# One z slot of the delta mixer computed together with the decay inputs, ahead of the mixer's rounds

## The reference, cut to what matters

```
x = rms_norm(x, norm_out_g)                        # end of the first block
h = rms_norm_2(x, g_mix)
proj = h @ w_in                                    # 1024 x 8224
glu_a, glu_b, q, k, v, z, a_in, b_in, gate_a, gate_b = split_cols(proj, IN_SIZES)
...                                                # short convolution and silu of q, k, v
g = -exp(a_log) * softplus(a_in + dt_bias)         # 2 x 8 decay inputs a token
beta = sigmoid(b_in)                               # 2 x 8 more
o = gated_delta_rule(forwards) + gated_delta_rule(backwards)   # 8 heads of 128
o = rms_norm_2(o, delta_norm_g) * silu(z)          # z: 1024 columns
```

## Time and profile before

| | us |
|---|---|
| median of three runs | 1200.44 (1199.74 to 1205.01) |
| the profiled execution, its own time | 1202.45 |
| its span, first to last instruction | 1200.5 |

### The profile page before, as it was taken

The page is one execution under the profiler, slowest core; times in us unless marked ns, Lnnn a source line. Parts: engine busy times, 40 slices in busy tenths (PEclk is TensorE's granted clock), DMA queues, the critical chain, the costliest instruction groups (busy, mean ns, idle before and its releaser), DMA issues.

```text
span 1200.5 us, 21345 instructions
## 1 busy us (share of the span) xinstructions
PE 1170.7 (98%) x8592; PEld 1087.1 (91%) x8592; DVE 839.9 (70%) x1519; ACT 700.9 (58%) x1181; POOL 324.8 (27%) x257
## 2 busy tenths in 40 slices
PE   8999999999999999999999999999999999999997
PEld 7777899998887799998899999999989989999886
DVE  6796588884675578885558787888854656555456
ACT  5475576663467576664466666776666445444344
POOL 1172200000027300000157667576555220000010
PEclk9999999999999999999989999999999999999999
DMA  7633355545543365555333332332323646555542
GB/s 286 251 141 140 128 211 207 195 181 204 179 183 133 120 246 211 209 184 213 134 141 140 107 133 98 124 125 87 105 72 108 226 176 221 209 186 201 202 154 82
DMA packets 31587, 199.74 MB, mean 166 GB/s; under 512 B 4289, under 2 KB 6481, under 8 KB 8706
## 3 DMA queue, kind: packets, MB, share of 16 engines
q1 hardware_dynamic: 29506, 189.27, 44.1%
q0 software_dynamic: 1840, 8.60, 1.8%
q10 hardware_dynamic: 144, 0.52, 0.1%
HBM read 197.33 MB, written 1.05 MB: 165 GB/s over the span
## 4 chain that ended last, share of the span: by engine, by line
PE 83%; DVE 9%; ACT 4%; issue 2%; POOL 1%; DMA 0%; SPq 0%; POOLq 0%; ACTq 0%; DVEq 0%
PE ps L1185 24%; PE ps L1187 23%; PE ps L1186 23%; PE ps L1562 1%; PE ps L1578 1%; DVE ps L2837 1%; PE ps L1339 1%; PE ps L1358 1%; DVE conv L2768 1%; PE ps L1326 1%; DVE wlo L2382 1%; PE ps L1210 1%; PE ps L1279 1%; DVE x L2511 1%; PE ps L1584 0%
## 5 line engine op out<-in xcount | busy, mean ns | idle before, releaser
L1185 PE MATMUL ps<-halves,whi 128*128 128x256 f32 x1472 | 411.1, 279 | 0.1
L1186 PE MATMUL ps<-halves,whi 128*128 128x256 f32 x1472 | 406.0, 276 | 0.0
L1187 PE MATMUL ps<-halves,wlo 128*128 128x256 f32 x1472 | 406.0, 276 | 0.0
L2382 DVE TENSOR_TENSOR wlo<-raw,whi 128x2048 fp32r<-128x2048 f32 (+1 forms) x133 | 300.6, 2263 | 116.1 <-ACT whi L1842 112.9
L1842 ACT ACTIVATE whi<-raw 128x2048 fp32r<-128x2048 f32 (+1 forms) x143 | 269.4, 1886 | 96.7 <-PE ps L1187 91.4
L1185 PEld LDWEIGHTS ps<-halves,whi 128*128 128x128 f32 x1472 | 283.8, 193 | 0.8 <-DVE halves L2976 0.5
L1187 PEld LDWEIGHTS ps<-halves,wlo 128*128 128x128 f32 x1472 | 283.8, 193 | 0.0
L1186 PEld LDWEIGHTS ps<-halves,whi 128*128 128x128 f32 x1472 | 283.8, 193 | 0.1
L1109 POOL TENSOR_TENSOR wlo<-raw,whi 128x1024 fp32r<-128x1024 f32 x72 | 172.4, 2404 | 53.4 <-ACT whi L1851 52.9
L1001 POOL TENSOR_TENSOR rstd<-sumsq,half_power 128x1 f32<-128x1 f32 x14 | 11.5, 824 | 573.2 <-ACT xn L1869 405.7
L1185 PE MATMUL ps<-whi,halves 128*128 128x512 f32 (+4 forms) x440 | 148.5, 337 | 4.1 <-DVE halves L2485 3.2
(11 more groups left out here) (337 smaller groups left out, 1847.0 us busy)
## 6 DMA issues: line engine op xcount, KB each, us to landing
raw<-in_stream SPq DMA_DIRECT2D x176, 1024.0 KB, 4.8
gain<-in_gains POOLq DMA_DIRECT2D x7, 512.0 KB, 6.0
bias<-in_rel POOLq DMA_DIRECT2D x1, 1536.0 KB, 8.4
raw<-in_stream SPq DMA_DIRECT2D x2, 648.0 KB, 7.3
cst<-in_consts POOLq DMA_DIRECT2D x1, 1280.5 KB, 9.1
raw<-in_stream SPq DMA_DIRECT2D x2, 528.0 KB, 4.4
x<-in_x SPq DMA_DIRECT2D x2, 512.0 KB, 4.3
out<-xn SPq DMA_DIRECT2D x4, 256.0 KB, 2.4
```

The source lines that it names most:

```text
L1185: nc.tensor.matmul(out, a_hi, b_hi, start=start, stop=False)
L1186: nc.tensor.matmul(out, a_hi, b_lo, start=False, stop=False)
L1187: return nc.tensor.matmul(out, a_lo, b_hi, start=False, stop=stop)
L2382: dve.tensor_tensor(used(wlo, n), used(raw, n), used(whi, n).bitcast(F32), ALU.subtract)\
```

## The change

The slot `z0` (256 columns of w_in) and the 32 decay columns become one matrix of 288 columns, in two "columns" slots of 512 rows each, `("z_decay", 0)` and `("z_decay", 1)`. They stand where `ab` stood. The number of slots stays the same. Its products are 48 matmuls of 288 columns, into bank 4 (t = 0) and bank 5 (t = 1). `decay_inputs` reads columns 256 to 287 of the two banks; the tanh and product of z0 (`first_z`) are issued in tick 7 of round 0 on ACT and DVE. The order of the other slots moves up, so that round 4 has three slots.

The splits move with it: ACT and DVE split one slot more in `norm_behind_down(4)`, DVE both halves of the new matrix ahead of the addition for t = 1 and its half of the first q-k slot at the very end; POOL's half of that slot comes behind both deviations and two memsets.

```diff
-    plan.append(("narrow", "ab", ("w_in_2", 0), 6144, 32))
+    rows_major("z_decay", ("w_in_2", 0), [(5120, 2 * P), (6144, 32)])
...
-    other = [glu[0:2], [z[0]] + glu[2:4], [glu[4], z[1]], [z[2], glu[5], z[3]], [glu[6], gates[0]],
+    other = [glu[0:2], glu[2:4] + [z[1]], [glu[4], z[2]], [glu[5], z[3], gates[0]], [glu[6]],
              [glu[7]] + gates[1:2], gates[2:3], gates[3:5]]
...
 POOL, double norm:
             for t in range(TT):
                 deviation(4, t)
                 deviation_5(t)
-                if t == 0:
-                    split_shared(("qk", 0))
             pool.memset(sum_row[:, :].bitcast(F32), 0.0).then_inc(*S["rows_cleared"].one("mixer"))
             pool.memset(glu_in[:, :, :], 0.0).then_inc(*S["glu_cleared"].one())
+            split_shared(("qk", 0))
...
 PE, in place of ab_products:
+            def first_z_and_decay_products(t):
+                for half in range(2):
+                    n = slot_of[("z_decay", half)]
+                    if t == 0:
+                        wait_low(pe, n)
+                    wait_split(5, t, (half,))
+                    wh, wl = used(whi, n), used(wlo, n)
+                    for i in range(4):
+                        kt = 4 * half + i
+                        last = three(ps[:, 4 + t, 0:Z_DECAY], xhi[:, kt, t * P:(t + 1) * P], xlo[:, kt, t * P:(t + 1) * P],
+                                     in_order(wh[:, i, :]), in_order(wl[:, i, :]), kt == 0, kt == KT - 1)
+                    if t:
+                        last.then_inc(*S["weights_used"].one(n))
...
             def level_turn(h):
                 pe.wait_ge(*S["inverse_begun"].at(h))
+                if h == 0:
+                    pe.wait_ge(*S["tanh_used"].at(("z", 0)))
...
 ACT, norm_behind_down:
                 split(last + 3)
                 round_turned(5 if k == 4 else k, [(1, 0), (1, 1)])
+                if k == 4:
+                    split(last + 4)
...
 DVE, norm_behind_down:
                 normalize(after, [0])
                 split(last + 1)
-                if k == 2:
+                if k in (2, 4):
                     split(last + 2)
                 add_to_x(k, last, 1)
...
                 lows(after, [(1, 0), (1, 1)])
+                if k == 4:
+                    split(last + 3)
...
 DVE, in tick 7 of round 0 (ACT makes the tanh before it):
+            def first_z():
+                dve.wait_ge(*S["tanh_made"].at(("z", 0)))
+                dve.scalar_tensor_tensor(xn[:, :, 0:TOK], tanh[:, TANH_OF[("z", 0)], :].rearrange("p (t c) -> p t c", t=2), 1.0,
+                                         ps[:, 4:6, 0:2 * P], ALU.add, ALU.mult).then_inc(*S["tanh_used"].one(("z", 0)))
```

More of the change, by code:

```diff
@@ L175, in pack_stream @@
                 out[n].reshape(P, KT, 2 * P)[:] = evens_first(out[n].reshape(P, KT, 2 * P))
-        elif kind == "narrow":
-            a, c = args
-            out[n].reshape(P, KT, 256)[:, :, 0:c] = w[:, a:a + c].reshape(KT, P, c).transpose(1, 0, 2)
         elif kind == "down":
@@ L547 @@
 AB_SPINS = (6, 2)
+Z_DECAY = 2 * P + 32
 END_SPINS = (5, 8)
@@ L556 @@
 NORMS = len(GAINS) - 1
-MIX_SLOTS = [("ab", -1, 0)] + [(slot[0], r, 2 * i) for r, slots in enumerate(ROUNDS) for i, slot in enumerate(slots)] \
+MIX_SLOTS = [(("z", 0), -1, 0)] + [(slot[0], r, 2 * i) for r, slots in enumerate(ROUNDS) for i, slot in enumerate(slots)] \
     + [(("delta_out", i), len(ROUNDS), 0) for i in range(KT // 2)]
@@ L580, in finished_slot @@
     return slot_at(r, i - 1) if i else slot_at(r - 1, TICKS - 1)
+FIRST_Z_AT = (0, 7)
 def tanh_order():
@@ L590, in tanh_order @@
                 order.append(key)
+            if (r, i) == FIRST_Z_AT:
+                order.append(("z", 0))
             if r < HEADS and i == 3:
@@ L820, in weights_of @@
                 return at.rearrange("p (k c) -> p k c", k=4)[:, :, 0:sum(c for _, c in entry[3])]
-            if entry[0] == "narrow":
-                return at.rearrange("p (k c) -> p k c", k=KT)[:, :, 0:entry[4]]
             return at
@@ L1772, in _ @@
                 turn_norm(5, t)
-                ab_products(t)
+                first_z_and_decay_products(t)
                 if t == 0:
@@ L2052, in up2 @@
                     .then_inc(*S["p_high"].one())
+            def first_z():
+                act.wait_ge(*S["weights_used"].at(slot_of[("z_decay", 1)]))
+                act.wait_ge(*tanh_free(TANH_BEFORE[("z", 0)]))
+                act.activation(tanh[:, TANH_OF[("z", 0)], :].rearrange("p (t c) -> p t c", t=2), ps[:, 4:6, 0:2 * P], ACT.Tanh,
+                               scale=0.5).then_inc(*S["tanh_made"].one(("z", 0)))
             def evacuate(key):
@@ L2296, in _ @@
                         evacuate(finished_slot(r, i))
+                    if (r, i) == FIRST_Z_AT:
+                        first_z()
                     if r < HEADS and i == 3:
@@ L2713, in decay_inputs @@
             def decay_inputs():
-                dve.wait_ge(*S["weights_used"].at(slot_of["ab"]))
+                dve.wait_ge(*S["weights_used"].at(slot_of[("z_decay", 1)]))
                 dve.wait_ge(params2_loaded, 16)
-                link(dve.tensor_copy(ab[:, 0, :, :], ps[:, 3, 0:64].rearrange("p (t c) -> p t c", t=2)))
+                link(dve.tensor_copy(ab[:, 0, :, :], ps[:, 4:6, 2 * P:Z_DECAY]))
                 dt = row_at["dt_bias_2"].unsqueeze(1).broadcast_to([P, TT, 16])
@@ L3027, in _ @@
             decay_inputs()
-            split(slot_of["ab"] + AHEAD)
+            split(slot_of[("z_decay", 1)] + AHEAD)
             for r in range(len(ROUNDS)):
```

## The result

The changed kernel is slower by 0.2%: 1206.06 us median of 20 executions against 1203.36 us for 20 of the kernel before, ratio 1.0021 [1.0012, 1.0031]. The forecast was 1197.7, with 1193.5 to 1202.5 as its range. It was wrong: in size and in sign against the kernel before.

A forecast was written before the change was run, and what follows sets the result against it. PE, busy 98% of the span, was taken as the bound. Norm with clock -0.8, z0's tanh and product +0.6, rounds 4 and 5 -2.5 sum to -2.7 us: 1197.7 us against the median, range 1193.5 to 1202.5.

The forecast's parts named there:

- The fall of the clock over t = 0: Double norm: one short clock fall after PE's 3.45 us idle stretch, costing 1.1 us, within bounds of 0 and 7 us.
- Part 4: Round 0, tick 7: z0's tanh and product added on ACT and DVE delay round 1; +0.6 us, from 0 to +0.69.
- Part 5: Rounds 4 and 5: round 4 loses a slot, round 5 gives some back; together -2.5 us, from -1.85 to -2.6.
- What hides the moved splits: Double norm: the moved q-k and v0 splits finish before PE wants them; v0 hidden by 1.8 us, no cost.
- What follows is a chain of latencies ... and moves along with it: From qk0's end to the next transposes: the chain shifts with qk0's end, keeping the 1.9 us full-clock gain.
- Part 3, the clock: Double norm: PE's idle stretch may lower the clock; 1.1 us taken, leaving -0.8 us for norm with clock.
- What would show it: Signs of error: matmul above 0.13 us, late q-k split, over 0.7 us extra round 1 wait, rounds 4-5 saving outside 1.5-4.
- PE starves at the norm and the clock falls for good: Double norm: first product 2.25 us late, half clock through both tiles; +2.5 us in all, 1202.9 us; chance 0.15.
- rival 3: Another name for "PE starves at the norm and the clock falls for good", the slower case; 1202.9 us, chance 0.15.

The follow-up runs named there:

- e6_first_spins: Changed kernel with only 14 spins on PE ahead of the t = 0 products at the double norm; ratio to the kernel before 0.9998.
- e2_rounds_only: Kernel before's double norm with the changed kernel's slot order in the rounds, z0 left out altogether; ratio to the kernel before 0.9985.
- e8_act_tail: Changed kernel plus 14 and 3 spins; ACT makes decay logarithms and evacuates qk0 before its half roundings, one POOL half split a tick later; ratio to before 1.0031.
- e9_tail: e7_late_half with qk0 evacuated ahead of glu0's second half, glu1's first-half remainders on DVE after the gating, three spins less; ratio to before 0.9961.
- e7_late_half: Changed kernel with DVE's split of the new matrix's second half behind t = 1's first gain, and spins at both waits; ratio to before 0.9977.
- e4_spins: Changed kernel with 14 spins ahead of the t = 0 products and 9 ahead of PE's wait for the first gated projection; ratio to before 0.9987.
- e5_wide_ab: Kernel before with its decay matmuls 256 columns wide instead of 32, the further columns unread; ratio to before 1.0005.
- e1: Changed kernel's double norm with the kernel before's rounds; z0 computed in the norm unread, and again in round 1; ratio to before 1.0040.
- e3: Changed kernel with ACT's decay logarithms a tick earlier and both halves of glu0's rounding behind qk0's evacuation; ratio to before 1.0056.
- e12: e9_tail run again unchanged, on one chip with e11; 1197.22 us, ratio to the kernel before 0.9955.
- e11: Kernel before with 256-column decay matmuls, spins ahead of the gated-projection wait and e9_tail's two tail moves, without the change; 1198.11 us, ratio 0.9959.

## Why the prediction was wrong

**Right.** The 288-column matmuls go in steps of 0.1225 us (609.00 to 611.45 us is twenty steps); 0.123 was forecast. PE's first product came at T + 4.42, 2.18 later than before; forecast 2.25, by the two splits on DVE (2.62 us; forecast 2.70). The row of after:

```profile
595.92 2.62 DVE L2396 TENSOR_TENSOR wlo<-raw,whi 128x1152 fp32r<-128x1152 f32 x2
```

The fall of the clock over t = 0, held possible behind the long idle stretch, came: the products took from 600.49 to 605.17, and e6_first_spins puts its cost at 1.04 us; forecast 1.1. Up to qk0's end the norm gained 0.9 us against before; forecast 0.8. This gain is the second low stretch of the earlier trace rows, which did not come over qk0 again; in e2_rounds_only an unchanged norm has only one such stretch, so the gain depends on the execution compared with. POOL's half of the q-k slot took 2.60 us, not the long 4.20, and was done at 608.24, ahead of PE's want at 611.57.

"Part 4" said +0.6: +0.32. DVE comes with the first `prod` of round 1 0.6 us later, and PE's wait at L1565 is 1.00 against 0.39; half of that is made up within the round. "Part 5" said -2.5: round 4 gave 2.49, round 5 took 0.80 back, together -1.69, just outside the bounds of -1.85 to -2.6; the missing part is in round 4, forecast at -2.9 to -3.7.

**Wrong, first step.** "What hides the moved splits" said of v0: ACT rounds it at 607.5 to 609.4, hidden by 1.8. It was held against PE's want of v0 alone. It came at 610.36 and hid there, but it pushed all that stands behind it in ACT's list: glu0's half, the three table loads, glu0's other half, qk0's evacuation. The sentence "What follows is a chain of latencies ... and moves along with it" assumed that PE's end of qk0 starts this chain; after the change ACT's queue does. Worth: PE 0.9 ahead at qk0's end, 0.74 behind at L1493, so 1.6 us. That it is this queue is shown by e8_act_tail, where the evacuation goes ahead of the halves and the same transposes come 1.51 us earlier; e9_tail against e7_late_half (0.94 us, with the evacuation and one remainder moved and three spins less) agrees. How the 1.6 divide between v0's rounding and the order of glu0's halves wasn't tried alone, and is argued from the rows.

**Wrong, second step.** "Part 3, the clock" looked for falls in the norm and priced one. It missed that a new wait at L1493 is also an idle stretch. The clock fell behind it for 6.9 us; from L1493 to round 1's turn PE took 21.77 us, before 18.59: +3.18. e4_spins and e6_first_spins show it: the same wait with spins in it costs 1.58 us less even where the fall was already halved. None of the signs that "What would show it" gave for being wrong came true (0.1225 us a matmul, no wait for the q-k split, 0.61 us more wait in round 1, 1.69 us saved): none of them looked at what lies between qk0's end and round 1.

Together: -0.89 + 1.63 + 3.18 = +3.92, then +0.32 and -1.69: +2.5. Of the 5.2 us between this and the forecast's -2.7, the two steps hold 4.8. The rival "PE starves at the norm and the clock falls for good" gave +2.5 and 1202.9, by half clock through both tiles. That the size agrees is chance, for the place was another: t = 1 ran at full clock throughout.

**A smaller error.** "Half of rival 3 lies at the end of the range" left the slower side thin: the three runs shown of before had a median of 1200.44, and the 20 executions that these three belong to 1203.36. The range of 1202.5 would have excluded the kernel before itself.

## What to carry to other kernels

When a step is moved on an engine, follow that engine's list to the next thing that the bound engine waits for; being done before its own consumer is not enough. And price every new wait of PE twice: its own length, and what the clock takes from the dense work behind it; spins in the wait bought that back here (2.65 and 1.58 us). Compare a change with a kernel that has the same cover: the clock's 4 us hid a change worth 0.6.

## What the runs showed of the hardware

- A matmul of 32 columns and one of 256 both step by 0.111 us, each with its own weight load (widening the decay products in e5_wide_ab lengthened nothing); 288 columns take 0.1225.
- PE idle for 3.38 us was followed by a granted clock of 0.50 over the next dense stretch, and so was a wait of only 2.02 us at L1493. Of the profiles, the five with an unfilled wait of 1.68 us or more at this place (after, e1, e3, e5, e6) have a stretch at 0.50 there. The seven with spins in it (e4, e7 to e12) and the two with a wait of 0.39 and 0.38 us (before, e2) have none there. Behind the 2.13 us idle of PE that ends at 110.09 us, where the stretch of the earlier trace rows ends, and with the same instructions, the clock is 1.00 from 110 to 113.5 us in the profile of before and 0.52 in that of after: it differs between executions, and that row was no safe bound.
- Two DVE gating instructions, 0.76 us together, took 4.54 (e3) and 4.97 us (e8) together beside POOL's splits; a POOL half split, 2.36 us alone, took 3.87 in after, where a DVE split of 2.29 us had begun 0.64 us ahead of it.
- The end of the span behind the last turn of the rounds is 319.9 us in ten profiles and 319.0 in four (e2, e9, e11, e12), with PE's last matmul at the same place in the pair compared (e7, e12); the difference lies in the last output's tail and isn't explained.
